# Expert blocks of 96 rows on four column groups of TensorE, in a two-block network on one core

## The reference

```python
x = first_block(x, mem, positions, ...)
qa, ka, va, qb, kb, vb, rb, gb, qn, kn, vn = split_in(h @ w_in)       # gb: 32 columns, the decay inputs
z = gl[..., direction * 16:(direction + 1) * 16] @ w_dec[direction] + b_dec[direction]
yb = gla_mixer(...)                                                   # gated linear attention, both directions
x = x + mod[:, 2] * (concatenate([ya, yb, yn], -1) @ w_out)
# experts: 32 of them, 2 for each token, 2048 rows in all, sorted by expert and padded to blocks
def expert_block(xb, e):
    g, u = jnp.split(xb @ w_up[e], 2, axis=-1)                        # 1024 -> 2 x 512
    return (jax.nn.silu(g) * u) @ w_down[e]                           # 512 -> 1024
x = x + mod[:, 5] * segment_sum(y * gate, token)
```

## Time and profile before

| | |
|---|---|
| median of 3 runs | 3420.76 us (3420.44 to 3423.78) |
| profiled execution | 3419.75 us |
| its span, first to last instruction | 3417.9 us |
| TensorE busy | 3252.6 us, 95% |
| VectorE, ScalarE busy | 1246.8 us, 890.6 us |
| experts stage, first product to last | 2652.7 to 3366 us |
| DMA traffic | 406.07 MB |

### The profile page before, as it was taken

One profiled execution on the slowest core, in us unless ns is written; L12 is line 12 of the kernel. 1 busy time (PEld: TensorE's weight loads), 2 busy tenths in 40 slices (PEclk: granted clock), 3 DMA queues, 4 the chain that ended last, 5 costly groups with the idle time before them and its releaser, 6 DMA issues. The chain is left out here.

```text
span 3417.9 us, 26806 instructions
## 1 busy us (share of the span) xinstructions
PE 3252.6 (95%) x10208; PEld 1578.3 (46%) x10208; DVE 1246.8 (36%) x1598; ACT 890.6 (26%) x1571; POOL 90.7 (3%) x106
## 2 busy tenths in 40 slices
PE   9998998999999998999999989978997999999997
PEld 4343443444444443444455445554464444444444
DVE  7834763233333333443210047664655011111113
ACT  2111773011111113343100036554312211111111
POOL 0000000000000000000000000030000000000002
PEclk9999999999999999999999999979978999999998
DMA  3114702101111104332321000011002988988874
GB/s 125 49 39 110 229 1 99 42 32 42 37 37 37 37 25 163 143 125 100 86 51 36 0 1 1 2 48 71 21 3 112 358 332 340 343 333 334 332 295 180
DMA packets 101972, 406.07 MB, mean 119 GB/s; under 512 B 7632, under 2 KB 8048, under 8 KB 97136
## 3 DMA queue, kind: packets, MB, share of 16 engines
q1 hardware_dynamic: 90208, 362.22, 29.4%
q0 software_dynamic: 7056, 25.69, 2.0%
q10 hardware_dynamic: 4608, 16.78, 1.2%
HBM read 367.96 MB, written 54.53 MB: 124 GB/s over the span
## 5 line engine op out<-in xcount | busy, mean ns | idle before, releaser
L2551 PE MATMUL ex_up_ps<-big,ex_xT 128*128 128x512 f32 x1024 | 452.7, 595 | 3.0 <-ACT ex_xT L2611 3.0
L1199 PE MATMUL fm_ring<-V,fm_up 128*128 128x512 f32 x704 | 316.6, 592 | 0.0
L1199 PE MATMUL fm_ring<-fm_n,fm_up 128*128 128x512 f32 x704 | 316.5, 592 | 0.0
L1428 PE MATMUL dn_acc<-big,V 128*128 128x512 f32 x704 | 305.4, 596 | 1.6 <-PEq L43 1.6
L2551 PEld LDWEIGHTS ex_up_ps<-big,ex_xT 128*128 128x128 f32 x1024 | 193.1, 191 | 234.2 <-issue 230.8
L1448 PE MATMUL dn_acc<-h,dn_tail 128*128 128x512 f32 x544 | 235.6, 592 | 0.0
L2570 PE MATMUL ex_y_ps<-ex_wd,ex_hT 128*128 128x512 f32 x512 | 227.7, 598 | 6.0 <-DVE ex_hT L2660 6.0
L1428 PEld LDWEIGHTS dn_acc<-big,V 128*128 128x128 f32 x704 | 134.6, 191 | 170.7 <-issue 170.7
L1199 PEld LDWEIGHTS fm_ring<-fm_n,fm_up 128*128 128x128 f32 x704 | 133.8, 190 | 168.4 <-issue 168.4
L1199 PEld LDWEIGHTS fm_ring<-V,fm_up 128*128 128x128 f32 x704 | 133.7, 190 | 167.9 <-issue 167.9
L678 PE MATMUL f_acc<-h,f_w 128*128 128x512 f32 x416 | 182.4, 598 | 0.0
(11 more groups left out here) (442 smaller groups left out, 3859.2 us busy)
## 6 DMA issues: line engine op xcount, KB each, us to landing
big<-in_w_eup SPq DMA_DIRECT2D x32, 4096.0 KB
ex_wd<-in_w_edown SPq DMA_DIRECT2D x32, 2048.0 KB, 13.1
y_dram<-in_cos SPq DMA_DIRECT2D x1, 24576.0 KB, 83.1
fm_up<-in_w_up SPq DMA_DIRECT2D x22, 1028.0 KB, 4.8
dn_tail<-in_w_mod SPq DMA_DIRECT2D x32, 512.0 KB, 7.1
y_dram<-big ACTq DMA_DIRECT2D x32, 512.0 KB, 7.8
V<-in_w_down SPq DMA_DIRECT2D x8, 1408.0 KB, 6.8
dn_tail<-in_w_in SPq DMA_DIRECT2D x17, 512.0 KB, 3.8
```

What stands on the lines that cost most here:

```text
L1199: mm = nc.tensor.matmul(slot(x)[:, a:a + BANK], up[:, i % 2, (2 * k + s) * P:(2 * k + s + 1) * P], n[k][:, a:a + BANK], start=(k == 0), st ...
L1428: mm = nc.tensor.matmul(o[:, x * BANK:(x + 1) * BANK], wd[j % 2][:, k * P:(k + 1) * P], hidden[:, k, x * BANK:(x + 1) * BANK], start=(k == ...
L2551: mm = nc.tensor.matmul(up_ps[:, s, :], xT[:, u, k, :], wu[:, u, k, s * H:(s + 1) * H], start=(k == 0), stop=(k == KD - 1))
```

## The change

A block holds `BR` = 96 rows in place of 128, in `GR` = 3 groups of 32, and there is room for 56 blocks in place of 48. In the products the rows are the stationary side, 32 columns for each matmul. Row group g writes partitions 32g to 32g + 31 with the first 384 columns of a bank; the last 128 columns of all three groups go to partitions 96 to 127, side by side. So each step of k is six matmuls on four column groups of 32. The hidden rows, `gate5` and `y` have the same layout; turning the hidden rows takes three transposes, and the store of a block three transfers. The up weights are loaded as two transfers, gate columns and value columns, each with a semaphore of its own, and each refilled as soon as its own product is done.

The two other edits: tile 7 of the second projection runs with 32 stationary columns, k modulo 4 choosing the column group, and `w_dec` is repeated four times so that the next matmul adds the groups up. In the linear attention the decay weights are loaded during the attention before, the parts are dealt out anew (four before the units, halves of parts between units, two in the tail), `sum_up(0)` comes before the second part's addition, and ScalarE does a first square root ahead of the tail.

```diff
 def load_up(...):
-    sp.dma_start(wu[:, u], din["w_eup"][bass.ds(e, 1)].rearrange(...)).then_inc(u_ready[u], 16)
+    n = slice(s * 512, s * 512 + 512)
+    sp.dma_start(wu[:, u, :, n], din["w_eup"][bass.ds(e, 1), :, n].rearrange(...)).then_inc(ready[2 * u + s], 16)
...
                 def load_gate_up(i, u):
                     e = expert_of(sp, r, i * 2 + u)
+                    if not isinstance(i, int):
+                        sp.wait_ge(gate_done, i * 2 + (u - 1))
+                    load_up(sp, din, e, wu, u, 0, u_ready)
                     sp.wait_ge(up_done, i * 2 + (u + 1))
-                    load_up(sp, din, e, wu, u, u_ready)
+                    load_up(sp, din, e, wu, u, 1, u_ready)
...
+                def grouped(o, rows, w, first, last):
+                    for g in range(GR):
+                        nc.tensor.matmul(o[32 * g:32 * g + 32, 0:W], rows(g), w[:, 0:W], start=first, stop=last)
+                    for g in range(GR):
+                        mm = nc.tensor.matmul(o[BR:P, g * P:(g + 1) * P], rows(g), w[:, W:BANK], start=first and g == 0,
+                                              stop=last and g == GR - 1)
+                    return mm
...
-                        mm = nc.tensor.transpose(x_ps[:, k, :], xb[:, u, k * P:(k + 1) * P], cst["ident"])
+                        mm = nc.tensor.transpose(x_ps[:, k, 0:BR], xb[0:BR, u, k * P:(k + 1) * P], cst["ident"][0:BR, 0:BR])
...
                 def product(i, u, s):
                     if s == 0:
                         pe.wait_ge(xT_ready, i * 2 + (u + 2))
-                        pe.wait_ge(u_ready[u], i * 16 + 16)
                         pe.wait_ge(silu_done, i * 2 + (u + 1))
+                    pe.wait_ge(u_ready[2 * u + s], i * 16 + 16)
                     for k in range(KD):
-                        mm = nc.tensor.matmul(up_ps[:, s, :], xT[:, u, k, :], wu[:, u, k, s * H:(s + 1) * H],
-                                              start=(k == 0), stop=(k == KD - 1))
+                        mm = grouped(up_ps[:, s, :], lambda g: xT[:, u, k, 32 * g:32 * g + 32], wu[:, u, k, s * H:(s + 1) * H],
+                                     k == 0, k == KD - 1)
...
                 def store_y(i, u):
-                    act.dma_start(y_dram[bass.ds(i * 2 + u, 1)].rearrange("a p n -> p (a n)"),
-                                  y[:, u, :]).then_inc(stored[u], 16)
+                    act.dma_start(dst[:, :, 0:W], y[0:BR, u]).then_inc(stored[u], 16)
+                    for c in range(2):
+                        act.dma_start(dst[:, c, W:BANK].rearrange("(g p) n -> p g n", g=GR),
+                                      y[BR:P, u, c].rearrange("p (g n) -> p g n", g=GR)).then_inc(stored[u], 16)
...
+                def narrow_or_wide(c, k, o, a, weights, src):
+                    n = src.shape[-1]
+                    if c == LOW:
+                        g = 32 * (k % 4)
+                        return nc.tensor.matmul(o[g:g + 32, a:a + n], weights[:, 0:32], src, start=(k < 4), stop=(k >= 4))
+                    return nc.tensor.matmul(o[:, a:a + n], weights, src, start=(k == 0), stop=(k == KD - 1))
...
-                part(0)
-                part(1)
-                for u in range(4):
-                    unit(0, u)
-                for i in range(2, 7):
+                for i in range(4):
                     part(i)
+                unit(0, 0)
+                unit(0, 1)
+                part(4, (0,))
+                unit(0, 2)
+                unit(0, 3)
+                part(4, (1,))
...
                     for u in range(4):
                         unit(n, u)
-                        if u == 1:
-                            part(8 + n)
+                        if u % 2:
+                            part(6 + n, (u // 2,))
...
+                part(14, (0,))
                 for i in range(2):
                     pe.wait_ge(squared, i + 1)
```

More of the change, by code:

```diff
@@ L1463, in _ @@
                         for k in range(KD):
-                            mm = nc.tensor.matmul(acc[:, pos["q", order[y]] % 2, T:T + NCTX], wq[:, y % 4, k, :], nctx[:, k, :],
-                                                  start=(k == 0), stop=(k == KD - 1))
+                            mm = narrow_or_wide(order[y], k, acc[:, pos["q", order[y]] % 2, :], T, wq[:, y % 4, k, :],
+                                                nctx[:, k, :])
                     mm.then_inc(done, 1)
@@ L1693 @@
 E_ = 32
-NB = 48
+BR = 96
+GR = BR // 32
+NB = 56
 NBI = NB + 1
@@ L1729, in gla_and_out @@
     out, gate = pr[:, 6:8, :], pr[:, 15:17, :]
-    w_dec, b_dec, gain = din["w_dec"], vecs["b_dec"], vecs["gla_g"]
+    b_dec, gain = vecs["b_dec"], vecs["gla_g"]
     n_out = 2 * KD
@@ L1807, in _, with part @@
             def _(pe):
-                def part(i):
+                def part(i, halves=(0, 1)):
                     j, x = i // 2, i % 2
-                    if x == 0:
+                    if halves[0] == 0:
                         pe.wait_ge(wa_ready[place[j]], 16 * (place[:j].count(place[j]) + 1))
-                    if i >= 2:
-                        pe.wait_ge(part_added, i - 1)
+                        if i >= 2:
+                            pe.wait_ge(part_added, i - 1)
                     for y, src in enumerate(others):
+                        if y // 3 not in halves:
+                            continue
                         mm = nc.tensor.matmul(ps[:, 6 + i % 2, :], wa[place[j]][:, y, :], src[:, x * BANK:(x + 1) * BANK],
                                               start=(y == 0), stop=(y == len(others) - 1))
-                    mm.then_inc(part_done, 1)
+                    if halves[-1] == 1:
+                        mm.then_inc(part_done, 1)
                 def unit(n, u):
@@ L1880, in _ @@
                     if j in (5, 11):
-                        part(7 + (j == 11))
+                        part(5 + (j == 11))
                 for n in range(1, N + 1):
@@ L1911, in _ @@
                     mm.then_inc(summed, 1)
+                part(14, (1,))
+                part(15, (0,))
                 for i in range(2):
@@ L1916, in _ @@
                     mm.then_inc(spread, 1)
+                part(15, (1,))
             @block.scalar
@@ L1980, in _ @@
                     nc.scalar.activation(sq[:, i, :], out[:, i, :], ACT.Square).then_inc(squared, 1)
+                nc.scalar.activation(decay[:, 0, :], cst["lane"][:, 0:C], ACT.Sqrt)
                 for i in range(2):
@@ L2197, in _ @@
                 sp.wait_ge(first_ready, 1)
-                load_up(sp, din, sp.value_load(r["first"][0:1, 0:1], min_val=0, max_val=E_ - 1), wu, 0, u_ready)
+                first = sp.value_load(r["first"][0:1, 0:1], min_val=0, max_val=E_ - 1)
+                for s in range(2):
+                    load_up(sp, din, first, wu, 0, s, u_ready)
                 for u in range(NR):
@@ L2558, in turn_hidden @@
                     pe.wait_ge(hT_ready, i * 2 + (u + 1))
-                    for k in range(KH):
+                    for k in range(GR):
                         mm = nc.tensor.transpose(h_ps[:, k, :], hid[:, 1, k * P:(k + 1) * P], cst["ident"])
@@ L2567, in down, with rows @@
                     pe.wait_ge(y_kept, i * 2 + (u + 1))
-                    for a, w in chunks(D):
+                    for c in range(2):
                         for k in range(KH):
-                            mm = nc.tensor.matmul(y_ps[:, a:a + w], hT[:, k, :], wd[:, u, k, a:a + w], start=(k == 0),
-                                                  stop=(k == KH - 1))
+                            def rows(g):
+                                return hT[:, k, 32 * g:32 * g + 32] if k < GR else hT[:, g, BR:P]
+                            mm = grouped(y_ps[:, c, :], rows, wd[:, u, k, c * BANK:(c + 1) * BANK], k == 0, k == KH - 1)
                     mm.then_inc(y_done, 1)
@@ L2963, in program @@
             w_o2_ready = [nc.alloc_semaphore(f"o2_w_ready{u}") for u in range(4)]
-            o2_first = Loads([(w_o2[u], din["w_out2a"][u].rearrange("p (k n) -> p k n", n=P), w_o2_ready[u]) for u in range(2)])
+            dec_in = nc.alloc_semaphore("dec_in")
+            w_dec = flat[:, 17 * T + 6 * P:18 * T].rearrange("p (d n) -> p d n", d=2)
+            o2_first = Loads([(w_dec, din["w_dec"], dec_in)] + [(w_o2[u], din["w_out2a"][u].rearrange("p (k n) -> p k n", n=P), w_o2_ready[u]) for u in range(2)])
             second_block(nc, din, cst, vecs, h, mod, neg_lam, sub_g[:], pr, pc, v2, vr, o2_first)
-            experts_block(nc, din, cst, vecs, h, h_dram, mod, a2[:], big, pc, vr, V, (w_o2, w_o2_ready), y_dram, y_filled, out, stack)
+            experts_block(nc, din, cst, vecs, h, h_dram, mod, a2[:], big, pc, vr, V, (w_o2, w_o2_ready), dec_in, y_dram, y_filled, out, stack)
 VECS = [("mix_g", KD), ("mem_g", KD), ("ffn_g", KD), ("q_g", 10), ("mk_g", 2),
```

112 lines of the change are left out of this document (60 added, 52 removed).

## The result

The changed kernel takes 3246.86 us, the median of 4 runs (3245.34 to 3253.75), where the kernel before took 3421.26 beside it. The ratio is 0.949 (0.948 to 0.951). The gain is 174 us; 116 were forecast, with a range that ended at 3262. The forecast was too cautious: the direction was right, but the gains that it gave the experts stage and the linear attention were too small.

The account below looks back on a forecast made before the run. TensorE was taken to set the pace, busy 95% of the span, with transfers close behind in the experts stage. 3419.75 - 96 (experts) - 12.4 (decay tile) - 8 (linear attention) + 1 (routing) = 3304, as median 3305 us; range 3262 to 3362.

Parts of the forecast that it names:

- TensorE's time in a block: Experts stage: 24 steps of 0.66 us, 1.2 for transposes and 0.36 for switches make 17.4 us a block.
- rival 3: Experts stage: column groups take turns, 1.52 us a step, 38.1 a block; 518 us lost, 3920; chance 0.13.
- The fetch at the loop's jump: Experts blocks loop: some 77 KB of code may wait for an instruction fetch, 0 to 1.6 us a block, 1.4 taken.
- The transfers: Experts stage: moving 7.08 MB a block takes 18.2 us, bounds 17.3 and 20.6.
- The 2 KB rows: Experts up load: pieces of 2 KB instead of 4 lengthen its 10.3 us by 0 to 1.9 us.
- the three stores: Experts block store: 384 pieces of 0.5 and 1.5 KB take 2.4 us and not 1.0, at most 1.4 more.
- The choice: Experts stage: the slower of TensorE and transfers paces the other; 18.9 us a block, saving 96 us.
- both middles: Experts stage: middles of the two block ranges, TensorE 17.4 to 19.0 us and transfers 17.3 to 20.6.
- The decay tile: Second projection, 17th column tile: four column groups cut 17.2 us to 4.7 with switches, 12.4 us saved.
- Linear attention: Early decay weights remove a 3.2 us wait, two output parts move to the tail; 8 us saved, from -2 to 12.
- Routing: Vector work over 56 block columns instead of 48, and a few small ScalarE copies: 1 us lost.
- the second: Experts stage: no fetch stall and 2 KB pieces free, block 18.0 us, 125 us saved, 3276; chance 0.15.

Follow-up runs that it names:

- the tile alone: Kernel before with only the narrow 17th column tile of the second projection on four column groups and decay products over 128 rows; 3404.17 us, ratio 0.995.
- the experts alone: Kernel before with only the change's experts stage: blocks of 96 rows on four column groups, up weights by halves, matching routing tables; 3281.36 us, ratio 0.960.

## Why the prediction was wrong

The sum was 3304 to 3305, 58 us too high: 42 of them lie in the experts stage (19 by the fetch, 16 by the price of the transfers, some 6 by two smaller parts of the choice), 11.5 in the linear attention, 1 in the routing, and some 3 in stages that the change does not touch. By its own steps, against the profiled spans:

- *TensorE's time in a block*, 17.4: 17.0. Right; the step is 0.645 us and not 0.66. That four column groups overlap at full rate, taken from the earlier trace rows with two, was right, and rival 3 with it wrong.
- *The fetch at the loop's jump*, 1.4 us a block, which made 17.4 into 18.8: nothing. **This step failed.** It was set between "nothing" and the wait of a small load, with a cold fetch thought likelier; no row bore on a loop that long, and the change stays within what TensorE keeps. It was no idle fear: at twice the length it costs about 12 us a turn. With it gone, the term behind it, the transfers, shows.
- *The transfers*, 18.2 from 17.3 to 20.6: 17.7. Within the bounds, off by 0.5; over 32 blocks that is 16 us. The 2 KB rows, priced at up to 1.9 us from short loads, cost 0.1; the three stores have no price that the runs separate.
- *The choice*, 18.9 a block, "just above both middles": 17.6 on average. Of the 1.3 us, 0.1 was the margin over the slower of the two, 18.8; 0.6 is the fetch, without which the slower was 18.2; 0.5 is the price of the transfers; and 0.1 are the first blocks, which run at TensorE's 17.0 on the transfers' lead. Two engines with double buffers between them don't add: 17.0 alone and 17.7 alone give 17.7 together. 96 us forecast, 138 to 140 measured.
- *The decay tile*, 12.4: 12.8.
- *Linear attention*, 8, from -2 to 12: 19.5. **The second step that failed**, by the size of the term, 11.5 us. The tail grew by 6.8, as the 5 to 8 forecast. The stretch ahead of the levels lost 24.2 us, where I had 3.2 and 0 to 10.6. The two parts at 5.3 us are 10.6 of it. TensorE's idle time in the stretch falls from 8.7 us to 5.2: 1.7 of the first wait, one of 0.9 and one of 3.0 for VectorE go, and one of 2.1 for VectorE is new. The other 10 us or so are clock: before, the first 48 passes of the parts and the decay products ahead of them took 33.3 us, now 25.1, which is 8 of them. I had priced passes at one clock, in a stage where the earlier trace rows gave 0.96 over a window that left the slow start out. The low clock stood in that start, at 0.67, and the first row tells of it: four passes in 3.78 us, where the earlier trace rows has 429 ns a pass.
- *Routing*, -1: 0 to 0.1. Wider tables of short instructions cost nothing that shows.

Of the rivals, the second (no fetch stall, 2 KB pieces free; 0.15) is what happened, and even it, at 18.0 a block, was 0.4 too slow: it kept a transfer time of its own guess. Its 3276 with the linear attention's real gain would have been 3264. The range ended at 3262, 15 us too high. Nor does that end come out of the prediction's own terms: 3276 with a linear attention of 12 in place of 8 is 3272. Another reading was off and entered no term: of a block of 21.90 us the DMA share of 0.88 leaves the engines 2.6 us, and 335 against 409 GB/s some 4, not 1.9.

Not settled: the stages between tile 7 and the linear attention take 3 us less in the changed kernel's profile, 5 less with the tile alone and none less with the experts alone. No instruction of theirs is changed, and the runs of one kernel differ by as much.

## What to carry to other kernels

When two resources run beside each other with double buffers, price each alone and take the slower one; don't add a margin for both being close, and test it by halving the load of either. Who sets the pace is read from the engine that does the work and from the rate, not from how long the issuing engine waits. Before costing passes from a row, look at the clock of that very stretch: a wait that goes, or a product over few rows that is widened, gives back the clock behind it too, here more than the wait itself. Narrow products that would leave columns idle can be packed on column groups, as long as neighbours in the program stand on different groups and the loop's code stays within what TensorE keeps: 77 KB was free, 153 KB cost about 12 us a turn, and nothing between was measured.

## What the runs showed of the hardware that was not expected

- Four column groups of 32, each over 128 rows in float32, run at full rate together: six passes in 0.32 us.
- TensorE starts passes for a free column group past some nine earlier ones; of 48 short passes behind 48 wide ones, nine started before the last wide ones.
- At the start of the linear attention, decay products over 32 rows let the granted clock fall to half while TensorE is fully busy (two profiles, 4.76 and 7.13 us for twelve passes); the same products over 128 rows do not (eight profiles, 4.37 us).
- Rows of 2 KB move at 401 GB/s, of 4 KB at 402, of 16 KB at 414, in streams of the same bytes (the 4 KB rows with whole refills).
- A jump back over 153 KB of code costs a wait of 5.8 us, another of 2.5, and half clock behind them; over 77 KB it costs nothing that shows (blocks of 17.00 us on both sides of the jump).
